# Spreading tokens into slots: 30 row masks with places of their own on GpSimd, and the clearing of `yo` and the identity behind them

## The chip, the cores and the metric

The kernel runs on one core of one Trainium2 chip. The metric is the device time of one execution in microseconds (us). The engines are TensorE (PE, with its weight loads PEld), VectorE (DVE), ScalarE (ACT), GpSimd (POOL) and SyncE (SP), which here only issues DMAs. Each works through its own instructions in order; semaphores tie them together.

## The reference

One layer of a streaming encoder over 2048 prompt tokens and 32 sample tokens, width 1024: a projection, a convolution group, stick-breaking attention, an output projection, and then a hierarchical mixture of experts, where the change lies. Each token picks one of 4 groups and two of its 8 experts; every expert is a SwiGLU block of hidden width 512.

```
lg = h @ w_rg; g_idx = argmax(lg); p_sel = softmax(lg)[g_idx]
le = (h @ w_re).reshape(T, 4, 8)[g_idx];  top_v, top_i = top_k(le, 2)
combine   = p_sel * softmax(top_v);  expert_id = g_idx * 8 + top_i
padded    = ceil(counts / 128) * 128                  # rows per expert, in blocks of 128
dest      = padded_start[expert] + rank within the expert
row_tok[dest] = token (T where empty);  row_w[dest] = combine weight
for each block of 128 rows, of expert e:
    y = (silu(x @ w_g[e]) * (x @ w_u[e])) @ w_d[e]
    out[row_tok] += y * row_w
```

## The kernel before

The program has three phases with a barrier between them: `phase_project`, `phase_attend` (its end also chooses experts and counts ranks, kept in `picks`) and `phase_moe`. Only `phase_moe` is touched.

`phase_moe` has an opening and then the experts. The opening turns, for each of 2080 tokens and two choices, the expert and the rank in it into a slot: block `col` and row `row` = rank mod 128. It is a *spread* by matmul: there are 34 pairs (2 choices by 17 tiles of 128 tokens). For each, a *row mask* (128 tokens by 128 rows, 1 where the token's row is that row) is the stationary operand and a *column mask* (128 tokens by 2 x 67 blocks, holding token number and weight at the token's block) the moving one; all 34 add up in the PSUM tile `up`, and give token and weight of every slot (`slots`).

- DVE first makes the table of the experts' first and last blocks (`nb`, `table`, L2090 to L2100), then casts `iota`, `tok` and `pad` (L2103 to L2105), then the row numbers (L2107 to L2110) and raises `rows_done`; then the column numbers (two products over 128x1088 and a sum, `oh`, `sel`, `col`), the weights (`vw`), and in the loop at L2128 the 34 column masks and every third row mask.
- POOL first makes the iotas, clears `yo` (L2197), builds the identity (L2198, L2200) and raises `zero_yo`; then it waits for `rows_done` and makes the other 23 row masks (L2210). Row and column masks have rings of `RS` = 6 buffers, so mask n waits until PE has done matmul n - 6. After `slots_done` it gathers the tokens of block 1 (it waits for `zeroed` there), then of block 2, and starts the scatter-adds to `y_out`.
- SP waits for `zero_yo`, stores the zeroed `yo` as the padding rows of `h2` and of `y_out` (semaphore `zeroed`), and then issues all weight loads, 12 pieces for each of 32 experts, in a ring of 16 buffers `raw`; a load waits until DVE has used the piece 16 before (`wlo_done`).
- ACT computes two exponentials, waits for `zero_yo`, then rounds the 12 pieces of expert 0 (`lead`, `w_hi`, L1949), and behind them rounds the transposed tokens of block 1 (`x_hi(1)`, L1953). DVE makes the remainders (`w_lo` L2152: five pieces, then `x_rest(1)` L2157, then the other seven).
- PE does the 34 matmuls (L1999), waits for `zero_yo`, transposes block 1 (L2007), and goes through the experts: per block `hidden` (up and gate, L2038), transposes of `h`, and `half_down` (L2027), three products for each pair of matrices.

No planner orders any of this; it is written out by hand, one queue per engine.

Of the kernel before, what the change touches and what calls it, by code (L numbers as in the profile page):

```python
# [16 lines left out]
P = 128  # L17
# [1800 lines left out]
def phase_moe(nc, io, scr, picks):  # L1818
# [6 lines left out]
    with ExitStack() as ctx:  # L1825
        def sb(name, shape, dt=F32):
            return ctx.enter_context(nc.sbuf_tensor("p3_" + name, shape, dt))
# [11 lines left out]
        NC = 2 * NT  # L1839
        se, psel, ex, den = (sb(x, [P, NT]) for x in ("se", "psel", "ex", "den"))  # L1840
        gx = sb("gx", [P, NT, NG])
# [8 lines left out]
        RS = 6  # L1850
        in_row, in_col = sb("in_row", [P, RS, P]), sb("in_col", [P, RS, 2, NBL])

# [32 lines left out]
        d_done, yo_done = sem("d_done"), sem("yo_done")  # L1885

        choices = [(k, r) for k in range(2) for r in range(NT)]
        pool_rows = [n for n in range(NC) if n % 3 < 2]

# [103 lines left out]
        def _(pe):  # L1993
            for n, (k, r) in enumerate(choices):
                m = DEC if ORDER[r] == PT else P
                if n in pool_rows:
                    pe.wait_ge(row_in, pool_rows.index(n) + 1)
                pe.wait_ge(spread_in, n + 1)
                pe.matmul(up[:, 0:2 * NBL], in_row[0:m, n % RS, :],  # L1999
                          in_col[0:m, n % RS, :, :].rearrange("p v b -> p (v b)"),  # L2000
                          start=(n == 0), stop=(n == len(choices) - 1)).then_inc(spread, 1)
# [71 lines left out]
        def _(dve):  # L2073
            links = [0]

            def link(ins):
                links[0] += 1
                ins.then_inc(chain, 1)
                dve.wait_ge(chain, links[0])

            def tt(out, a, b, op):
                link(dve.tensor_tensor(out, a, b, op))
# [4 lines left out]
            def flat(ap):  # L2087
                return ap.rearrange("p k t -> p (k t)")

            link(dve.tensor_scalar(nb[:, 0, :], picks.count, float(P - 1), None, ALU.add))  # L2090
            link(dve.tensor_copy(nbi[:, :], nb[:, 0, :]))
# [8 lines left out]
            dve.sem_inc(table_done, 1)  # L2100

            dve.wait_ge(consts, 5)
            link(dve.tensor_copy(iota[:, :], iota_i[:, :]))  # L2103
            link(dve.tensor_copy(tok[:, :], tok_i[:, :]))
            link(dve.tensor_copy(pad[:, :], pad_i[:, :]))  # L2105

            link(dve.tensor_copy(rki[:, :], flat(picks.rank)))  # L2107
            link(dve.tensor_scalar(rki[:, :], rki[:, :], 7, None, ALU.logical_shift_right))
            link(dve.tensor_copy(hi[:, :], rki[:, :]))
            link(dve.scalar_tensor_tensor(row[:, :], hi[:, :], -float(P), flat(picks.rank), ALU.mult, ALU.add))  # L2110
            dve.sem_inc(rows_done, 1)
            tt(oh[:, :, :], iota[:, 0:NE].unsqueeze(1).broadcast_to([P, NC, NE]), over(flat(picks.expert), NE),
# [6 lines left out]
            link(dve.tensor_reduce(se[:, :], gx[:, :, :], AX.X, ALU.add))  # L2119
            link(dve.reciprocal(psel[:, :], se[:, :]))  # L2120
            link(dve.tensor_scalar_add(den[:, :], ex[:, :], 1.0))
            link(dve.reciprocal(se[:, :], den[:, :]))
            for k in range(2):
                tt(vw[:, k * NT:(k + 1) * NT, 0], tok[:, :], row[:, k * NT:(k + 1) * NT], ALU.subtract)
            tt(vw[:, 0:NT, 1], se[:, :], psel[:, :], ALU.mult)
            tt(vw[:, NT:NC, 1], vw[:, 0:NT, 1], ex[:, :], ALU.mult)

            for n in range(NC):  # L2128
                if n >= RS:
                    dve.wait_ge(spread, n - RS + 1)  # L2130
                if n not in pool_rows:
                    dve.tensor_scalar(in_row[:, n % RS, :], iota[:, :], row[:, n:n + 1], None, ALU.is_equal)
                dve.scalar_tensor_tensor(in_col[:, n % RS, :, :],
                                         iota[:, 0:NBL].unsqueeze(1).broadcast_to([P, 2, NBL]), col[:, n:n + 1],
                                         vw[:, n, :].unsqueeze(2).broadcast_to([P, 2, NBL]), ALU.is_equal,
                                         ALU.mult).then_inc(spread_in, 1)
# [53 lines left out]
        def _(pool):  # L2190
            pool.iota(iota_i[:, :], pattern=[[1, P]], base=0, channel_multiplier=0).then_inc(consts, 1)
            at = ORDER.index(PT)
            for lo, n, first in ((0, at, 0), (at, 1, PT), (at + 1, NT - at - 1, at)):
                pool.iota(tok_i[:, lo:lo + n], pattern=[[P, n]], base=first * P - PAD,
                          channel_multiplier=1).then_inc(consts, 1)
            pool.iota(pad_i[:, :], pattern=[[0, 1]], base=PAD, channel_multiplier=1).then_inc(consts, 1)
            pool.memset(yo[:, :], 0.0).then_inc(consts, 1)  # L2197
            pool.memset(ident[:, :], 0.0).then_inc(ident_done, 1)  # L2198
# [5 lines left out]
            pool.sem_inc(zero_yo, 1)  # L2204

            pool.wait_ge(rows_done, 1)
            for n in pool_rows:
                if n >= RS:
                    pool.wait_ge(spread, n - RS + 1)
                pool.tensor_scalar(in_row[:, n % RS, :], iota[:, :], row[:, n:n + 1], None,  # L2210
                                   ALU.is_equal).then_inc(row_in, 1)

# [107 lines left out]
```

## Time and profile before

| what | us |
|---|---|
| median of 3 runs | 2269.47 (2268.47 to 2271.46) |
| the profiled execution | 2268.2 |
| its span, first to last instruction | 2266.5 |
| PE, DVE, ACT, POOL busy | 2132.9, 1634.1, 1296.8, 745.0 |
| third phase begins | 1350.0 |

Times inside the span count from its start. "busy" on PE is matmuls that overlap one another, so it says how rarely PE is empty, not how near to its peak it is. The chain that ended last takes 34% of the span on PE, 3% on ACT and 1% each on DVE and POOL in the page's own grouping. The opening of the third phase, from 1350.0 to the first expert matmul at 1387.3, is 37 us of the 2266.5.

### The profile page before, as it was taken

What the parts mean: (1) busy time and instruction counts of PE and PEld (TensorE: products, weight loads), DVE (VectorE), ACT (ScalarE), POOL (GpSimd) and SP (SyncE); (2) the same over time, 40 slices, a digit from 0 to 9 for tenths busy, and PEclk for the clock granted to TensorE, in tenths of its full rate; (3) what the DMA queues carried; (4) which work ended last, traced back from release to release, by engine and by line L of the source; (5) the groups of instructions that cost most, each with busy time, mean ns of one, the idle gap of its engine ahead of it and who ended that gap; (6) DMA issues with size and microseconds to landing.
All of it is one profiled execution on the core that took longest, in us unless ns stands there. A gap on an engine that the chain in (4) does not pass through costs nothing. (4 is left out here: it accounts for less than half of the span.)

```text
span 2266.5 us, 39757 instructions
## 1 busy us (share of the span) xinstructions
PE 2132.9 (94%) x13278; PEld 1790.1 (79%) x13279; DVE 1634.1 (72%) x2215; ACT 1296.8 (57%) x2417; POOL 745.0 (33%) x681
## 2 busy tenths in 40 slices
PE   8999999995899999899999857999999999999997
PEld 6888888884687887678778646888888888888886
DVE  3798999984676667877888868688688466466633
ACT  5222433335677677767767625588688465465533
POOL 1110444552466655544444423111111111111111
PEclk9999999996999999999999978999999999999999
DMA  6542433335433242332222129999899778678852
GB/s 219 198 163 85 137 118 112 118 115 176 120 103 106 80 140 75 107 110 91 78 101 71 61 88 342 331 334 377 290 377 375 247 231 273 219 236 278 276 171 46
DMA packets 209242, 406.60 MB, mean 179 GB/s; under 512 B 50623, under 2 KB 77119, under 8 KB 209117
## 3 DMA queue, kind: packets, MB, share of 16 engines
q1 hardware_dynamic: 195581, 355.71, 44.8%
q0 software_dynamic: 13536, 49.29, 9.2%
q8 instruction: 70, 1.15, 0.2%
q14 instruction: 55, 0.45, 0.1%
HBM read 312.27 MB, written 92.67 MB: 179 GB/s over the span
## 5 line engine op out<-in xcount | busy, mean ns | idle before, releaser
L2152 DVE TENSOR_TENSOR p_w_lo<-p_raw,p_w_hi 128x1024 fp32r<-128x1024 f32 x384 | 446.0, 1220 | 181.7 <-ACT p_w_hi L1949 181.0
L1792 POOL TENSOR_TENSOR p_wgt<-p_wgt,p_past 128x1024 f32<-128x1024 f32 (+4 forms) x166 | 308.4, 1859 | 350.5 <-DVE p_past L1670 347.4
L1949 ACT ACTIVATE p_w_hi<-p_raw 128x1024 fp32r<-128x1024 f32 x384 | 377.4, 1053 | 62.3 <-PE p_up L2038 51.8
L559 DVE SCALAR_TENSOR_TENSOR p_ut<-p_ut,p_cw 128x512 f32<-128x512 f32 (+1 forms) x480 | 329.2, 765 | 0.0
L1670 DVE TENSOR_TENSOR_SCAN p_past<-p_keep,p_past,p_one 128x513 f32<-128x513 f32 (+1 forms) x196 | 225.9, 1193 | 75.1 <-ACT p_keep L1481 73.1
L298 PE MATMUL p_pj<-p_w_hi,p_xt_hi 128*128 128x512 f32 x680 | 270.8, 398 | 4.2 <-DVE p_xt_lo L535 2.4
L298 PE MATMUL p_pj<-p_w_hi,p_xt_lo 128*128 128x512 f32 x680 | 266.3, 392 | 0.0
L298 PE MATMUL p_pj<-p_w_lo,p_xt_hi 128*128 128x512 f32 x680 | 265.8, 391 | 0.0
L1481 ACT ACTIVATE p_keep<-p_zp 128x512 f32<-128x512 f32 (+3 forms) x326 | 158.8, 547 | 118.1 <-PE p_zp L1351 105.4
L2038 PE MATMUL p_gp<-p_w_lo,p_xt_hi 128*128 128x256 f32 x736 | 206.7, 281 | 0.0
L2038 PE MATMUL p_gp<-p_w_hi,p_xt_lo 128*128 128x256 f32 x736 | 206.7, 281 | 0.0
L2038 PE MATMUL p_gp<-p_w_hi,p_xt_hi 128*128 128x256 f32 x736 | 206.6, 281 | 0.0
L1494 ACT ACTIVATE p_at<-p_tp 128x512 f32<-128x512 f32 (+3 forms) x261 | 134.2, 564 | 61.8 <-PE p_tp L1361 61.3
L2229 POOL DMA_INDIRECT y_out<-p_yo,p_at_s x47 | 75.5, 1606 | 284.1 <-ACT p_yo L1978 283.8
L1486 ACT ACTIVATE p_wgt<-p_zp 128x512 f32<-128x512 f32 (+3 forms) x326 | 160.2, 562 | 0.0
L1361 PE MATMUL p_tp<-p_ident,p_wgt 128*128 128x128 f32 x1106 | 151.4, 276 | 6.9 <-DVE p_at L1683 6.1
L1389 PE MATMUL p_op<-p_at,p_v 128*64 128x128 f32 x2176 | 155.2, 281 | 0.0
L2027 PE MATMUL p_dp<-p_w_hi,p_ht_hi 128*128 128x512 f32 x368 | 149.0, 405 | 4.3
L298 PEld LDWEIGHTS p_pj<-p_w_hi,p_xt_hi 128*128 128x128 f32 x680 | 128.3, 189 | 30.4 <-DVE p_xt_lo L535 2.8
L1670 DVE TENSOR_TENSOR_SCAN p_past<-p_keep,p_one 128x385 f32<-128x385 f32 (+3 forms) x130 | 113.9, 918 | 49.9 <-ACT p_keep L1481 46.2
L298 PEld LDWEIGHTS p_pj<-p_w_hi,p_xt_lo 128*128 128x128 f32 x680 | 128.1, 188 | 27.4
L2038 PE MATMUL p_up<-p_w_hi,p_xt_hi 128*128 128x512 f32 x368 | 146.3, 398 | 2.7 <-DVE p_xt_lo L2157 2.7
(268 smaller groups left out, 4713.2 us busy)
## 6 DMA issues: line engine op xcount, KB each, us to landing
p_raw<-in_w_up SPq DMA_DIRECT2D x128, 512.0 KB
p_raw<-in_w_gate SPq DMA_DIRECT2D x128, 512.0 KB
p_raw<-in_w_down SPq DMA_DIRECT2D x128, 512.0 KB
p_w_raw<-in_w_in SPq DMA_DIRECT2D x40, 256.0 KB, 3.8
p_x<-in_x SPq DMA_DIRECT2D x17, 512.0 KB, 4.1
p_y<-in_x SPq DMA_DIRECT2D x17, 512.0 KB
scr_y<-p_y SPq DMA_DIRECT2D x17, 512.0 KB, 3.0
p_y<-scr_y SPq DMA_DIRECT2D x17, 512.0 KB
```

The lines of the kernel that those rows point to most:

```text
L298: last = pe.matmul(pj[:, n % NPJ, :], xa[:, b, k, :], wa[:, place[c], k, :], start=(m == 0), stop=(m == 3 * KT - 1))
L559: dve.scalar_tensor_tensor(dst, src, cw[:, a, j:j + 1], dst, ALU.mult, ALU.add).then_inc(tap_done, 1)
L1361: end = pe.transpose(tp[:, n % 2, b * P:(b + 1) * P], wgt[:, u % NW, x * HW + b * P:x * HW + (b + 1) * P], ident[:, :])
L1389: end = pe.matmul(op[x * HD:(x + 1) * HD, pair * P:(pair + 1) * P], v_sb[:, key_slot(g, kt), h * HD:(h + 1) * HD], at[:, (base[u] + x) % N ...
L1481: act.activation(keep_rows[:, u % NK, x, HW - w:HW], zp[:, (base[u] + x) % NZ, 0:w], ACT.Sigmoid, scale=-SCALE).then_inc(keep_done, 1)
L1486: act.activation(wgt[:, u % NW, x * HW:x * HW + w], zp[:, (base[u] + x) % NZ, 0:w], ACT.Sigmoid, scale=SCALE).then_inc(sig_done, 1)
L1670: end = dve.tensor_tensor_scan(past[:, u % NP, to + w + 1:to:-1], src, one[:, 0:1].broadcast_to([P, w + 1]), past[:, (u - 1) % NP, to + 1: ...
L1792: pool.tensor_tensor(mine, mine, past_rows[:, u % NP, 0:n, 2:2 + w], ALU.mult).then_inc(a_done, 1)
L1949: act.activation(w_hi[:, p, :], raw[:, n % RING, :], ACT.Copy).then_inc(whi_done, 1)
L2027: last = pe.matmul(dp[:, c, :], ha[:, f, :], wa[:, KT + f, c * 512:(c + 1) * 512], start=(start and n == 0), stop=(not start and n == 5))
L2038: last = pe.matmul(dst, xa[:, k, :], wa[:, piece, at + lo:at + hi], start=(n == 0), stop=(n == 3 * KT - 1))
L2152: dve.tensor_tensor(w_lo[:, p, :], raw[:, n % RING, :], w_hi[:, p, :].bitcast(F32), ALU.subtract).then_inc(wlo_done, 1)
```

## The change

What it does:

- The 34 row masks lose their ring of six. There are 30 places: eight 128-column pieces of `xg`, eight of `yo`, four of `h`, four of `sg` and six of `in_rows`; mask n goes to place n mod 30. The tiles borrowed are used by the experts later. Column masks keep their ring of six.
- POOL makes 30 of the 34 row masks (`n % 7 < 6`) instead of 23, DVE 4 instead of 11. From mask 30 on POOL waits until matmul n - 30 is done.
- DVE works out the row numbers and casts `iota` first, raises `rows_done`, and then makes the table. `tok` and `pad` are cast after the column numbers. The weight is one reciprocal of (ex + 1) * se instead of two reciprocals and a product.
- POOL makes its masks right after the iotas. Clearing `yo` and building the identity, and with them `zero_yo`, stand behind the masks and a wait for the first 16 matmuls (the masks in `yo` have then been read). The code of SP and ACT is as it was.

```diff
--- before.py
+++ after.py
@@ -1837,7 +1837,7 @@
 
         iota_i, iota = sb("iota_i", [P, P], I32), sb("iota", [P, P])
         NC = 2 * NT
-        se, psel, ex, den = (sb(x, [P, NT]) for x in ("se", "psel", "ex", "den"))
+        se, ex, den = (sb(x, [P, NT]) for x in ("se", "ex", "den"))
         gx = sb("gx", [P, NT, NG])
         oh, sel = sb("oh", [P, NC, NE]), sb("sel", [P, NC])
         rki, hi = sb("rki", [P, NC], I32), sb("hi", [P, NC])
@@ -1848,7 +1848,7 @@
         nb, nbi = sb("nb", [P, 2, NE]), sb("nbi", [P, NE], I32)
         table = sb("table", [1, 2, NE], I32)
         RS = 6
-        in_row, in_col = sb("in_row", [P, RS, P]), sb("in_col", [P, RS, 2, NBL])
+        in_rows, in_col = sb("in_rows", [P, RS * P]), sb("in_col", [P, RS, 2, NBL])
 
         w_hi, w_lo = sb("w_hi", [P, PIECES, 2 * FF], F32R), sb("w_lo", [P, PIECES, 2 * FF], F32R)
         raw = sb("raw", [P, RING, 2 * FF])
@@ -1884,8 +1884,11 @@
         ht_ps, hh_done, hl_done = ([sem(f"{x}{i}") for i in range(2)] for x in ("ht_ps", "hh_done", "hl_done"))
         d_done, yo_done = sem("d_done"), sem("yo_done")
 
+        homes = [home[:, n * P:(n + 1) * P] for home, m in ((xg, 8), (yo, 8), (h, 4), (sg, 4), (in_rows, 6))
+                 for n in range(m)]
+        HOMES = len(homes)
         choices = [(k, r) for k in range(2) for r in range(NT)]
-        pool_rows = [n for n in range(NC) if n % 3 < 2]
+        pool_rows = [n for n in range(NC) if n % 7 < 6]
 
         block = ctx.enter_context(nc.Block())
 
@@ -1996,7 +1999,7 @@
                 if n in pool_rows:
                     pe.wait_ge(row_in, pool_rows.index(n) + 1)
                 pe.wait_ge(spread_in, n + 1)
-                pe.matmul(up[:, 0:2 * NBL], in_row[0:m, n % RS, :],
+                pe.matmul(up[:, 0:2 * NBL], homes[n % HOMES][0:m, :],
                           in_col[0:m, n % RS, :, :].rearrange("p v b -> p (v b)"),
                           start=(n == 0), stop=(n == len(choices) - 1)).then_inc(spread, 1)
 
@@ -2087,6 +2090,13 @@
             def flat(ap):
                 return ap.rearrange("p k t -> p (k t)")
 
+            link(dve.tensor_copy(rki[:, :], flat(picks.rank)))
+            link(dve.tensor_scalar(rki[:, :], rki[:, :], 7, None, ALU.logical_shift_right))
+            link(dve.tensor_copy(hi[:, :], rki[:, :]))
+            link(dve.scalar_tensor_tensor(row[:, :], hi[:, :], -float(P), flat(picks.rank), ALU.mult, ALU.add))
+            dve.wait_ge(consts, 5)
+            link(dve.tensor_copy(iota[:, :], iota_i[:, :]))
+            dve.sem_inc(rows_done, 1)
             link(dve.tensor_scalar(nb[:, 0, :], picks.count, float(P - 1), None, ALU.add))
             link(dve.tensor_copy(nbi[:, :], nb[:, 0, :]))
             link(dve.tensor_scalar(nbi[:, :], nbi[:, :], 7, None, ALU.logical_shift_right))
@@ -2098,17 +2108,6 @@
             link(dve.scalar_tensor_tensor(nb[0:1, 0, :], nb[0:1, 0, :], -1.0, nb[0:1, 1, :], ALU.add, ALU.add))
             link(dve.tensor_copy(table[0:1, 1, :], nb[0:1, 0, :]))
             dve.sem_inc(table_done, 1)
-
-            dve.wait_ge(consts, 5)
-            link(dve.tensor_copy(iota[:, :], iota_i[:, :]))
-            link(dve.tensor_copy(tok[:, :], tok_i[:, :]))
-            link(dve.tensor_copy(pad[:, :], pad_i[:, :]))
-
-            link(dve.tensor_copy(rki[:, :], flat(picks.rank)))
-            link(dve.tensor_scalar(rki[:, :], rki[:, :], 7, None, ALU.logical_shift_right))
-            link(dve.tensor_copy(hi[:, :], rki[:, :]))
-            link(dve.scalar_tensor_tensor(row[:, :], hi[:, :], -float(P), flat(picks.rank), ALU.mult, ALU.add))
-            dve.sem_inc(rows_done, 1)
             tt(oh[:, :, :], iota[:, 0:NE].unsqueeze(1).broadcast_to([P, NC, NE]), over(flat(picks.expert), NE),
                ALU.is_equal)
             tt(oh[:, :, :], oh[:, :, :], nb[:, 1, :].unsqueeze(1).broadcast_to([P, NC, NE]), ALU.mult)
@@ -2117,19 +2116,19 @@
 
             dve.wait_ge(exped, 1)
             link(dve.tensor_reduce(se[:, :], gx[:, :, :], AX.X, ALU.add))
-            link(dve.reciprocal(psel[:, :], se[:, :]))
-            link(dve.tensor_scalar_add(den[:, :], ex[:, :], 1.0))
-            link(dve.reciprocal(se[:, :], den[:, :]))
+            link(dve.scalar_tensor_tensor(den[:, :], ex[:, :], 1.0, se[:, :], ALU.add, ALU.mult))
+            link(dve.tensor_copy(tok[:, :], tok_i[:, :]))
+            link(dve.tensor_copy(pad[:, :], pad_i[:, :]))
             for k in range(2):
                 tt(vw[:, k * NT:(k + 1) * NT, 0], tok[:, :], row[:, k * NT:(k + 1) * NT], ALU.subtract)
-            tt(vw[:, 0:NT, 1], se[:, :], psel[:, :], ALU.mult)
+            link(dve.reciprocal(vw[:, 0:NT, 1], den[:, :]))
             tt(vw[:, NT:NC, 1], vw[:, 0:NT, 1], ex[:, :], ALU.mult)
 
             for n in range(NC):
                 if n >= RS:
                     dve.wait_ge(spread, n - RS + 1)
                 if n not in pool_rows:
-                    dve.tensor_scalar(in_row[:, n % RS, :], iota[:, :], row[:, n:n + 1], None, ALU.is_equal)
+                    dve.tensor_scalar(homes[n % HOMES], iota[:, :], row[:, n:n + 1], None, ALU.is_equal)
                 dve.scalar_tensor_tensor(in_col[:, n % RS, :, :],
                                          iota[:, 0:NBL].unsqueeze(1).broadcast_to([P, 2, NBL]), col[:, n:n + 1],
                                          vw[:, n, :].unsqueeze(2).broadcast_to([P, 2, NBL]), ALU.is_equal,
@@ -2194,6 +2193,14 @@
                 pool.iota(tok_i[:, lo:lo + n], pattern=[[P, n]], base=first * P - PAD,
                           channel_multiplier=1).then_inc(consts, 1)
             pool.iota(pad_i[:, :], pattern=[[0, 1]], base=PAD, channel_multiplier=1).then_inc(consts, 1)
+            pool.wait_ge(rows_done, 1)
+            for n in pool_rows:
+                if n >= HOMES:
+                    pool.wait_ge(spread, n - HOMES + 1)
+                pool.tensor_scalar(homes[n % HOMES], iota[:, :], row[:, n:n + 1], None,
+                                   ALU.is_equal).then_inc(row_in, 1)
+
+            pool.wait_ge(spread, 16)
             pool.memset(yo[:, :], 0.0).then_inc(consts, 1)
             pool.memset(ident[:, :], 0.0).then_inc(ident_done, 1)
             pool.wait_ge(ident_done, 1)
@@ -2202,13 +2209,6 @@
             pool.wait_ge(ident_done, 2)
             pool.wait_ge(consts, 6)
             pool.sem_inc(zero_yo, 1)
-
-            pool.wait_ge(rows_done, 1)
-            for n in pool_rows:
-                if n >= RS:
-                    pool.wait_ge(spread, n - RS + 1)
-                pool.tensor_scalar(in_row[:, n % RS, :], iota[:, :], row[:, n:n + 1], None,
-                                   ALU.is_equal).then_inc(row_in, 1)
 
             pool.wait_ge(slots_done, 1)
```

On POOL, at the opening of the third phase, before (`p_yo` and `p_ident` are the clearing and the identity, `p_in_row` the row masks, `p_at_g` and `p_xg` the first gather):

```order
L2191 IOTA p_iota_i 128x128
L2194 IOTA p_tok_i 128x6
L2194 IOTA p_tok_i 128x1
L2194 IOTA p_tok_i 128x10
L2196 IOTA p_pad_i 128x1
L2197 MEMSET p_yo 128x1024
L2198 MEMSET p_ident 128x128
L2200 AFFINE_SELECT p_ident<-p_ident 128x128
L2210 TENSOR_SCALAR p_in_row<-p_iota,p_row 128x128 x23
L2217 COPY p_at_g<-p_slots 128x1
L2219 DMA p_xg<-scr_h,p_at_g 128x1024
```

And now:

```order
L2195 IOTA p_pad_i 128x1
L2200 TENSOR_SCALAR p_xg<-p_iota,p_row 128x128 x7
L2200 TENSOR_SCALAR p_yo<-p_iota,p_row 128x128 x7
L2200 TENSOR_SCALAR p_h<-p_iota,p_row 128x128 x4
L2200 TENSOR_SCALAR p_sg<-p_iota,p_row 128x128 x3
L2200 TENSOR_SCALAR p_in_rows<-p_iota,p_row 128x128 x5
L2200 TENSOR_SCALAR p_xg<-p_iota,p_row 128x128 x4
L2204 MEMSET p_yo 128x1024
L2205 MEMSET p_ident 128x128
L2207 AFFINE_SELECT p_ident<-p_ident 128x128
L2217 COPY p_at_g<-p_slots 128x1
L2219 DMA p_xg<-scr_h,p_at_g 128x1024
```

The 30 masks have moved from behind the two memsets and the identity to ahead of them, and the masks' outputs are six tiles' pieces by turns.

On DVE, the start of the third phase, before (`p_nb`, `p_table` are the experts' table, `p_rki`, `p_hi`, `p_row` the row numbers; POOL's masks wait for the last of them and for `p_iota`):

```order
L2090 TENSOR_SCALAR p_nb<-picks 128x32
L2091 CAST p_nbi<-p_nb 128x32
L2092 TENSOR_SCALAR p_nbi<-p_nbi 128x32
...
L2099 CAST p_table<-p_nb 1x32
L2103 CAST p_iota<-p_iota_i 128x128
L2104 CAST p_tok<-p_tok_i 128x17
L2105 CAST p_pad<-p_pad_i 128x1
L2107 CAST p_rki<-picks 128x34
L2108 TENSOR_SCALAR p_rki<-p_rki 128x34
L2109 CAST p_hi<-p_rki 128x34
L2110 SCALAR_TENSOR_TENSOR p_row<-p_hi,picks 128x34
```

And now:

```order
L2093 CAST p_rki<-picks 128x34
L2094 TENSOR_SCALAR p_rki<-p_rki 128x34
L2095 CAST p_hi<-p_rki 128x34
L2096 SCALAR_TENSOR_TENSOR p_row<-p_hi,picks 128x34
L2098 CAST p_iota<-p_iota_i 128x128
L2100 TENSOR_SCALAR p_nb<-picks 128x32
L2101 CAST p_nbi<-p_nb 128x32
L2102 TENSOR_SCALAR p_nbi<-p_nbi 128x32
```

The row numbers and `p_iota` are the first five instructions instead of the last eight before the products.

## Rows read from the trace of the kernel before

**Rows 1.** Chain of waits, 1350 to 1430: start us, us, what
```profile
1375.21 1.09 PE p_up L1999 x6
...
1377.72 4.84 DMA p_xg<-scr_h,p_at_g
...
1387.27 7.26 PE p_up L2038 x24
...
1426.65 5.60 PE p_up L2038 x24
```

**Rows 2.** Windows, PE alone: stretch, its length, busy (instructions), granted clock, DMA share, GB/s
```profile
1400.00:1600.00 200.00, 196.39 (x1132) 1.00 0.98 342
1600.00:1800.00 200.00, 196.51 (x1157) 1.00 0.97 335
```

**Rows 3.** Timeline of ACT: start us, us, engine, line, operation [idle before, releaser]
```profile
1358.87 1.06 ACT L1949 ACTIVATE p_w_hi<-p_raw 128x1024 fp32r<-128x1024 f32 x1 [7.25 <-DMA p_raw<-in_w_up]
...
1373.64 1.06 ACT L1949 ACTIVATE p_w_hi<-p_raw 128x1024 fp32r<-128x1024 f32 x1 [0.25 <-DMA p_raw<-in_w_down]
1384.63 1.02 ACT L1953 ACTIVATE p_xt_hi<-p_xtp 128x1024 fp32r<-128x1024 f32 x1 [9.93 <-PE p_xtp L2007]
```

**Rows 4.** Timeline of SP's queue
```profile
1352.17 0.33 SPq L1910 DMA_DIRECT2D scr_h<-p_yo  x1
...
1353.02 3.19 SPq L1906 DMA_DIRECT2D p_raw<-in_w_up  x4
```

**Rows 5.** Timeline of POOL
```profile
1350.49 0.95 POOL L2197 MEMSET p_yo<- 128x1024 f32 x1
...
1351.77 0.29 POOL L2200 TENSOR_SCALAR_AFFINE_SELECT p_ident<-p_ident 128x128 f32<-128x128 f32 x1 [0.15 <-POOL p_ident L2198]
1354.83 4.29 POOL L2210 TENSOR_SCALAR p_in_row<-p_iota,p_row 128x128 f32<-128x128 f32 x4 [2.77 <-DVEq L2111]
1362.38 2.71 POOL L2210 TENSOR_SCALAR p_in_row<-p_iota,p_row 128x128 f32<-128x128 f32 x4 [3.26 <-PE p_up L1999]
1365.35 10.38 POOL L2210 TENSOR_SCALAR p_in_row<-p_iota,p_row 128x128 f32<-128x128 f32 x15 [0.26 <-PE p_up L1999]
```

**Rows 6.** Timeline of DVE
```profile
1350.50 0.98 DVE L2092 TENSOR_SCALAR p_nbi<-p_nbi 128x32 int32<-128x32 int32 x1
...
1353.16 0.23 DVE L2103 CAST p_iota<-p_iota_i 128x128 f32<-128x128 int32 x1
...
1353.82 0.18 DVE L2107 CAST p_rki<-picks 128x34 int32<-128x34 f32 x1
...
1354.47 0.20 DVE L2110 SCALAR_TENSOR_TENSOR p_row<-p_hi,picks 128x34 f32<-128x34 f32 x1
1354.82 1.29 DVE L2082 TENSOR_TENSOR p_oh<-p_iota,picks 128x1088 f32<-128x1088 f32 x1
...
1360.99 0.63 DVE L2133 SCALAR_TENSOR_TENSOR p_in_col<-p_iota,p_col,p_vw 128x134 f32<-128x134 f32 x2
```

**Rows 7.** Windows, PE alone, as rows 2
```profile
1361.00:1370.00 9.00, 8.50 (x36) 0.51 1.05 398
1370.00:1376.00 6.00, 5.42 (x34) 1.00 1.04 395
1387.00:1390.00 3.00, 2.73 (x7) 0.50 1.12 409
```

**Rows 8.** DMA issues: out<-in, queue, kind, count, KB, median us to landing
```profile
p_xg<-scr_h,p_at_g POOLq DMA_INDIRECT x47, 6.2
y_out<-p_yo,p_at_s POOLq DMA_INDIRECT x47, 9.0
...
y_out<-p_yo SPq DMA_DIRECT2D x1, 512.0 KB, 4.1
```

**Rows 9.** Masks by source, from 1365.6 and 1362: ns min/median/max, first and last start
```profile
L2133 DVE SCALAR_TENSOR_TENSOR p_in_col<-p_iota,p_col,p_vw x22: 344/351/462, 1365.4 to 1374.3; 128x134 f32<-128x134 f32 x22
...
L2210 POOL TENSOR_SCALAR p_in_row<-p_iota,p_row x19: 596/671/827, 1362.4 to 1375.1; 128x128 f32<-128x128 f32 x19
```

## The prediction

> **What bounds the kernel now.** I read the page first: TensorE (PE) is the engine with most busy time, and its matmul lines lead the chain. The change touches only the opening of the third phase (the experts), so the next view is the chain of waits from 1350 us on [rows 1]. It shows the phase opening with eleven microseconds of VectorE (DVE), then the spread (34 matmuls on PE, whose left operands, the row masks, come mostly from GpSimd, POOL), then the slot numbers, the gather of the first block's tokens, its transposition, the two halves of it (ACT, then DVE), and at 1387.27 the first expert matmul. From there on PE is what ends last: it is busy for 196.39 and 196.51 of the 200 us from 1400 and from 1600 [rows 2]. So a microsecond by which the first expert matmul moves is a microsecond of the kernel, but for at most 3.6 + 3.5 = 7.1 us of idle PE in those 400 us.
>
> Beside this chain runs a second one that the page does not list, because it ends earlier. ScalarE (ACT) rounds the first expert's 12 weight pieces (`lead`) before it does `x_hi(1)`, in one queue. The first of the 12 starts at 1358.87, the last at 1373.64, and `x_hi(1)` starts at 1384.63 [rows 3]: ACT has then been idle for 9.93 us. The 12 pieces come at 14.77 / 11 = 1.34 us each, although one takes ACT 1.06 us: the DMA sets the pace. Their loads are issued by SP from 1353.02, behind the two stores of the zeroed `yo` that begin at 1352.17 [rows 4], and SP starts all of this on `zero_yo`, which POOL raises when the memsets and the identity are done: memset of `yo` at 1350.49, identity finished at 1351.77 + 0.29 = 1352.06 [rows 5]. So the second chain has about ten microseconds of slack, and it hangs on POOL's clearing.
>
> **The change part by part.**
>
> *Row numbers first.* Before, POOL gets its first row mask at 1354.83, behind DVE's count chain, the three casts and the row numbers [rows 5, 6]. Now four operations 0.22 us apart, the last 0.2 long (1353.82 to 1354.67), and one cast of 0.26 (1353.16 to 1353.42) stand ahead: 1350.00 + 0.85 + 0.26 = 1351.1, and POOL starts 0.16 us later as it does before: 1351.3, 3.5 us earlier.
>
> *30 masks on POOL, none waiting for a buffer.* Before, POOL sits idle for 3.26 us before 1362.38 and 0.26 us before 1365.35, because the ring of six is full [rows 5]; that goes, since only the four masks from the 31st on still wait for PE, whose matmuls are long past. A mask on POOL takes 0.60 us at its shortest and 0.83 at its longest in the steady stretch [rows 9]. The first four, beside DVE's two 128x1088 products of 1.3 us, took 4.29 together, 1.9 more than 4 x 0.60; the last 15 in a row, beside the column masks, took 10.38, which is 0.692 each [rows 5, 6]. For 30: four around the products 4.3, about six more with DVE in small operations 3.6, and 20 at 0.692 13.8, together 21.7: the last mask ends at 1351.3 + 21.7 = 1373.0 where it ended at 1375.73. Bounds: 1371.2 if nothing but the products slows them (1.9 + 30 x 0.60 = 19.9), 1375.2 if the other 26 take 0.75 each, halfway between 0.67 (the median) and 0.83.
>
> *PE and DVE in the spread.* DVE's first column mask stood at 1360.99 [rows 6]. Ahead of it two small operations of some 0.25 us fall away, and 0.8 us of DVE's shift at 1350.50, which took 0.98 us beside POOL's memset where a like cast took 0.18: so PE can start near 1359.7. It has two matmul records per mask: 36 in the 9 us at the granted 0.51 (1.2 GHz), 34 in the 6 us at 2.4 GHz [rows 7], which is at most 0.50 and 0.35 per mask. About 18 go at half clock until 1368.7, 16 more take 5.6: PE could end at 1374.3, close behind POOL's last mask. I put the spread's end at 1374 instead of 1376.3 [rows 1]; that gain of some 2.3 us lies on the old chain only. DVE, with seven masks fewer, is no bound.
>
> *Clearing and identity behind the masks.* Nothing in SP's or ACT's code moves, but both open with a wait for `zero_yo`, and it now comes behind 30 masks. The clearing takes 1.57 us (1350.49 to 1352.06), so `zero_yo` comes at 1373.0 + 1.6 = 1374.6 instead of 1352.06: 22.5 us later. Queued behind that wait on SP are the two zero stores and all weight loads; on ACT the 12 roundings and `x_hi(1)`; PE waits for it too, after the spread. What waits for SP's stores is the gather (`zeroed`): the slower one lands 4.1 us after issue [rows 8], so at about 1375 + 4.1 = 1379, and gather 1 goes out about 1379.6, not 1377.72 [rows 1]. With 6.2 us to landing and the 2.07 us from there (1382.56) to `x_hi(1)`, the transposes, the block is there at 1388: still ahead of ACT.
>
> ACT's last rounding ended at 1373.64 + 1.06 = 1374.70 and so ends at 1374.70 + 22.5 = 1397.2 if the DMAs run as before. They do not quite: gather 1, gather 2 (out at about 1388.5) and the first scatter-add (about 1390) now fall into the same stretch, where before they came after it. A piece of 128x1024 numbers costs 1.34 us of the DMA's pace and a gather moves as many. Bounds: one such transfer (1.3) and four, counting the scatter-add twice (5.3). I take two and a half, 3.3, since the two gathers fall wholly and the scatter-add, 9.0 us to landing, partly, ahead of the last piece. So `x_hi(1)` starts at 1397.2 + 3.3 = 1400.5 instead of 1384.63: 15.9 us later. What follows is the same code: x_rest, PE, and DVE's second seven pieces, which stand behind x_rest and shift with it.
>
> *The clock.* The first 24 expert matmuls took 7.26 us where 24 later ones took 5.60 [rows 1], because the granted clock was 0.50 (1.2 GHz) for their first 3 us [rows 7]: 1.7 us. Now PE idles about twelve microseconds between the transposes and that point. The other low stretch in the rows, nine microseconds from 1361 after about 15 of idling, would do half the work and cost 4.5. So the extra lies between 0 and 2.8; I take 1.0, nearer to the row of the same matmuls.
>
> Sum: 15.9 + 1.0 = 16.9 us slower. The profiled execution took 2268.2 (span 2266.5 and 1.7 around it): 2285.1. The median of the runs is 1.3 us higher, 2269.47, so a median of about 2286.
>
> **The rivals.**
>
> *POOL is shut out by every column mask.* The masks beside the 1.3 us products lost 1.9 us, and DVE's shift beside the memset 0.8 [rows 5, 6]: the two engines do hold each other up. If each column mask of DVE, which reads two operands from SBUF as the products do, kept POOL out for its whole length, the 20 masks from 1359.8 on and the 34 column masks of 0.35 us would stand in line: 12.0 + 11.9 = 23.9 us, the last mask at 1383.7, `zero_yo` 10.7 us later still, 2297 for a median. Against it: from 1365.35 to 1375.73 POOL made 15 masks while DVE made 22 column masks [rows 9]; one after the other they need 15 x 0.60 + 22 x 0.35 = 16.7 us and had 10.4. 3%. The rule behind this rival is in the Trainium skill (SBUF — State Buffer, section on the two separate sides): VectorE and GpSimd share one port pair under an exclusive lock, which a VectorE operation with two SBUF inputs holds against a reading GpSimd operation for all of its length. The trace agrees with it for the long products (1.9 us lost) and not for the column masks (10.4 us where the rule needs 16.7).
>
> *Part is given back.* PE's 7.1 us of idle up to 1800 could shrink if what it waits for there runs on while PE is late. Against it: those waits are for ACT's and DVE's work on the running block, which shifts with it. At most 2286 - 7 = 2279. 6%.
>
> *The weight stream stays behind.* Loads start 22.5 us later and PE only 17, so the second expert's pieces may come late. By pace, the first 28 pieces (two experts and the third's up-weights) and eight other transfers need 36 x 1.34 = 48 us from 1375, until 1423. Before, PE began the third block's up-matmuls at 1426.65 [rows 1] and would now at 1443: a wide margin, unless the ring's releases chain badly: then 3 to 8 us more, 2289 to 2294. 6%.
>
> *The loads stay hidden: not slower.* Then only the old chain counts, with the spread's end 2.3 us earlier: 2269.47 - 2.3 = 2267. It decides where the 12 pieces are rounded within the 7 us or so between `zero_yo` at 1374.6 and the transposes, 0.6 us each; DMA gave 1.34 and ACT alone takes 1.06. Only if `zero_yo` came by about 1362 would the slack cover it, and 30 masks of 0.60 from 1351.3 exclude that. 3%, mostly for something I misread.
>
> That the masks are not made faster (POOL slowed all along) would not save the case: a spread that ends later makes `zero_yo` later too.
>
> **How the numbers follow.** 82% for the forecast with its own terms: low with the masks through at 1371.2 (1.8 less), one transfer (2.0 less) and no extra clock (1.0 less) 12.1, which is 2280.3 by the profiled execution; high with 1375.2 (2.2 more), four transfers (2.0 more) and 2.8 of clock (1.8 more) 22.9, which is 2291.1 by it and 2292.4 for a median. This range also holds most of the stream rival and some of the give-back; the lock rival stays out. About 0.2%, 4.5 us, is what a measurement can tell here from no change. Faster by more: 2%, within: 2%, slower: 96%.
>
> **What would show it.** In the changed profile: POOL's first mask near 1351.3, its last near 1373; memset of `yo` right behind it; SP's first store near 1375; ACT's 12 roundings from about 1381.5 to 1400, in a row, with idle time that ended with `p_raw` DMAs; the chain of waits through weight DMA and L1949 instead of the gather; the first expert matmul at 1403, at half clock; equal idle time of PE afterwards. It is wrong if ACT's `x_hi(1)` stands before 1395, if SP's loads start before POOL's masks are through, or if PE's idle time after 1400 (on the shifted scale) falls by several microseconds.

## The result and the profile after

The changed kernel takes 2283.62 us (median of 6 runs, 2282.68 to 2286.20), the kernel before 2269.43: a ratio of 1.0068 (95% interval 1.0057 to 1.0078), 14.2 us slower by the medians. (The ratios in this document are the estimates on record with their intervals, not the quotient of two medians; that is 1.0063 here and lies inside the interval.) The prediction was 2286, between 2280.3 and 2292.4. The profiled execution took 2282.77, its span is 2281.1.

One thing has to be known before the traces are laid side by side. The first two phases, whose code is the same, do not take equally long in every execution: the third phase begins at 1349.97 in the trace of before and at 1348.79 in that of after, and between 1348.40 and 1352.58 in those of the experiments. So I read everything from the start of the third phase (POOL's first iota), and compare *the length of the third phase*, span minus that start: 2266.5 - 1350.0 = 916.5 us before, 2281.1 - 1348.8 = 932.3 after, 15.8 us longer.

POOL's timeline after (start us, us, engine, line, operation) answers to [rows 5]:

```profile
1348.79 0.24 POOL L2190 IOTA p_iota_i<- 128x128 int32 x1 [15.88 <-POOLq L2260]
...
1350.15 6.06 POOL L2200 TENSOR_SCALAR p_xg<-p_iota,p_row 128x128 f32<-128x128 f32 x7 [0.78 <-DVEq L2099]
1356.19 4.13 POOL L2200 TENSOR_SCALAR p_yo<-p_iota,p_row 128x128 f32<-128x128 f32 x7
...
1367.82 2.64 POOL L2200 TENSOR_SCALAR p_xg<-p_iota,p_row 128x128 f32<-128x128 f32 x4
1370.41 0.95 POOL L2204 MEMSET p_yo<- 128x1024 f32 x1
...
1371.65 0.42 POOL L2207 TENSOR_SCALAR_AFFINE_SELECT p_ident<-p_ident 128x128 f32<-128x128 f32 x1
...
1377.61 1.26 POOL L2219 DMA_INDIRECT p_xg<-scr_h,p_at_g  x1 [0.64 <-POOL p_at_g L2217]
```

The masks start 1.36 us into the phase (4.86 before) and run without a gap to 21.67 (25.76 before); the clearing follows, and `zero_yo` comes at 1372.07, 23.3 us into the phase instead of 2.1. SP's queue follows at once [rows 4]:

```profile
1372.17 0.33 SPq L1913 DMA_DIRECT2D scr_h<-p_yo  x1
1372.54 0.43 SPq L1914 DMA_DIRECT2D y_out<-p_yo  x1
1373.02 3.18 SPq L1909 DMA_DIRECT2D p_raw<-in_w_up  x4
```

And ACT [rows 3], whose 9.93 us of idle time before `x_hi(1)` are gone:

```profile
1378.72 1.06 ACT L1952 ACTIVATE p_w_hi<-p_raw 128x1024 fp32r<-128x1024 f32 x1 [28.28 <-DMA p_raw<-in_w_up]
...
1394.30 1.06 ACT L1952 ACTIVATE p_w_hi<-p_raw 128x1024 fp32r<-128x1024 f32 x1 [0.86 <-DMA p_raw<-in_w_down]
1397.37 1.06 ACT L1952 ACTIVATE p_w_hi<-p_raw 128x1024 fp32r<-128x1024 f32 x1 [2.01 <-DMA p_raw<-in_w_down]
1398.33 1.01 ACT L1956 ACTIVATE p_xt_hi<-p_xtp 128x1024 fp32r<-128x1024 f32 x1
```

`x_hi(1)` now starts directly behind the last of the 12 roundings, and that one waited 2.01 us for its DMA. The chain of waits after (start us, us, what), where [rows 1] had the gather, now runs through the masks, the clearing, SP's queue and the weight load:

```profile
1370.46 0.89 POOL p_yo L2204
...
1382.05 0.52 SPq L1909
1382.62 14.73 DMA p_raw<-in_w_down
...
1398.33 1.02 ACT p_xt_hi L1956
1399.37 1.24 DVE p_xt_lo L2156
1400.61 0.34 issue
1400.95 8.28 PE p_up L2041 x24
```

The first 24 expert matmuls take 8.28 us instead of 7.26. Windows of PE (length, busy, granted clock, DMA share, GB/s) show the clock in that place, and PE's busy time later, 14 us on from the windows of [rows 2]:

```profile
1398.00:1401.00 3.00, 0.05 (x1) 0.50 1.02 383
1401.00:1404.00 3.00, 3.00 (x7) 0.50 1.04 391
1404.00:1407.00 3.00, 3.00 (x10) 0.61 1.06 391
```
```profile
1414.00:1614.00 200.00, 196.41 (x1135) 1.00 0.99 348
1614.00:1814.00 200.00, 196.55 (x1157) 1.00 0.96 333
```

196.41 and 196.55 where it was 196.39 and 196.51: nothing is given back later. From the phase's start, the first expert matmul moved from 37.30 to 52.16 us, 14.9 later, and the 24 took 1.0 longer: together 15.9, which accounts for the phase's 15.8. What follows the 24 takes 872.0 us before and 871.9 after, and between 871.6 and 872.4 in the traces of all the experiments: everything that differs between these kernels lies ahead of that point.

### The profile page after: what moved, and what is told of

Same layout as the page of the kernel before. It is cut to its first block and busy times, and to the rows that moved or that the text cites. A ratio compares the mean times of both kernels' runs of the same rounds, so it can differ in the third digit from the quotient of the medians.

```text
span 2281.1 us, 39763 instructions
## 1 busy us (share of the span) xinstructions
PE 2130.4 (93%) x13278; PEld 1788.8 (78%) x13279; DVE 1632.3 (72%) x2206; ACT 1298.4 (57%) x2417; POOL 746.1 (33%) x688
## 5 line engine op out<-in xcount | busy, mean ns | idle before, releaser
L2217 POOL COPY p_at_g<-p_slots 128x1 int32 (+1 forms) x47 | 9.5, 201 | 428.8 <-PE p_xtp L2010 424.0
```

## Experiments

The table has for each kernel the median, and from its trace, in us from the start of the third phase: SP's first store (just behind `zero_yo`), the last rounding's end, `x_hi(1)`, the first expert matmul; then the spread's end and the phase's length. In the edits, comment lines and `...` stand for code that is left out.

```
kernel                      median    store  rounded  x_hi(1)  matmul  spread  phase
before                      2269.43    2.20    24.7    34.7     37.3    26.3   916.5
after                       2283.62   23.38    49.6    49.5     52.2    24.1   932.3
1  clearing first           2267.11    2.25    24.7    32.9     35.6    24.7   915.5
2  before, clearing last    2286.46   26.16    52.1    52.0     54.6    25.1   935.1
3  loads ahead of the wait  2274.15   23.43    21.6    39.6     42.2    24.1   922.1
4  second gather late       2282.38   23.39    47.1    47.0     49.7    23.9   929.6
5  clearing at mask 10      2271.58   10.74    33.6    36.1     38.7    25.4   917.7
6  clearing at mask 20      2277.27   17.06    41.0    40.9     43.5    24.0   923.4
7  after, PE kept busy      2285.62   23.60    50.0    49.9     52.6    23.1   931.6
8  clearing first, PE busy  2264.48    2.25    25.0    32.5     35.1    24.2   912.7
9  split 23 and 11          2268.27    2.25    25.0    33.0     35.7    24.3   916.7
10 row numbers late         2268.56    2.19    25.0    34.1     36.8    25.6   915.9
```

There is one trace for each kernel, and two stretches in it differ between traces for no reason in the code. The first 24 expert matmuls take 7.26 to 8.63 us in the ten kernels whose TensorE is given no extra work, depending on when the granted clock rises from 0.50 (some 3 us after their start in the kernel before, some 5 in the first experiment); three kernels that leave TensorE idle for the same 2.7 us just ahead of them (the first, ninth and tenth) have 8.07, 8.60 and 7.53. The spread ends at 24.1 in three traces and at 23.1 in a fourth (the seventh), with the same masks made by the same engines in the same order. So a difference of less than about 1.4 us in the phase, or 1 us in the spread, is not shown by these traces alone; the column `matmul` is free of the first of the two.

### 1: the clearing first, all else as changed

```diff
-        in_rows, in_col = sb("in_rows", [P, RS * P]), ...
+        in_rows, in_col = sb("in_rows", [P, 14 * P]), ...
-        ... ((xg, 8), (yo, 8), (h, 4), (sg, 4), (in_rows, 6))
+        ... ((xg, 8), (h, 4), (sg, 4), (in_rows, 14))
 # POOL: memset yo, memset ident, affine_select, zero_yo
-# behind the 30 masks and wait_ge(spread, 16)
+# ahead of wait_ge(rows_done, 1) and the 30 masks
```

> The changed kernel with the clearing of yo and the identity ahead of the masks again; the eight places in yo are replaced by eight more in a tile of their own, so all 30 places, the 30:4 split and DVE's new order stay. My theory (the late zero_yo delays the weight loads, and nothing else in the change costs time): the loads start 3 us into the phase, are hidden, and only the faster spread is left: the first mask about 2.2 us into the phase, the last mask about 23, the spread's end about 24.5 instead of 26.3: 2267.5, 1.5 to 2 us below the kernel before. Rival (30 masks on GpSimd, or the borrowed places, cost the time): 2278 or more.

Measured: 2267.11 beside 2268.84 for the kernel before on the same chip, ratio 0.9993 (0.9984 to 1.0002). The interval holds no change; the phase is 1.0 us shorter than before, which is within the scatter, and 16.8 shorter than the changed one. First mask at 2.4, last mask's end at 22.3, spread's end at 24.7: within 0.7 us of what was expected. ACT waits for the transposes again, as in the kernel before:

```profile
1382.14 1.02 ACT L1956 ACTIVATE p_xt_hi<-p_xtp 128x1024 fp32r<-128x1024 f32 x1 [8.20 <-PE p_xtp L2010]
```

So 30 masks on POOL and the 16 places that are still borrowed cost nothing; the place of the clearing, which the eight places in `yo` force, costs all of it. The first matmul is 1.7 us earlier than before, and 0.8 of that goes again, since the first 24 take 8.07 us.

### 2: the kernel before with nothing but the clearing moved

```diff
+            # wait for rows_done, 23 masks
             pool.memset(yo[:, :], 0.0).then_inc(consts, 1)
             ...
             pool.sem_inc(zero_yo, 1)
-            # wait for rows_done, 23 masks
```

> The kernel before with one edit: the clearing and the identity, with zero_yo, moved behind its 23 masks. My theory: masks end 25.7 us into the phase, zero_yo at 27.3, the last rounding 26.4 later at 53.7, x_hi(1) 19 us later than before, and 1 us of half clock: 2289.5. Rival (the new masks cost the time, not the clearing): 2269 to 2270.

Measured: 2286.46, ratio 1.0073 (1.0057 to 1.0089), the phase 18.6 us longer than before. One edit, none of the rest, and the slowdown is there, with ACT waiting for a load up to the last piece:

```profile
1402.28 1.06 ACT L1949 ACTIVATE p_w_hi<-p_raw 128x1024 fp32r<-128x1024 f32 x1 [1.71 <-DMA p_raw<-in_w_down]
```

The phase grew by 1.4 us less than the 20.0 that 2289.5 stands for (the medians on this chip differ by 17.6). Most of this is that `zero_yo` came at 26.1, not 27.3: without the memset beside it DVE finishes the row numbers 0.8 us earlier, and 15 masks took 9.95 us instead of 10.38.

### 3: the late `zero_yo` kept, the first loads taken out of its wait

```diff
+            load(0, 0)
             sp.wait_ge(zero_yo, 1)
             ...stores...
-            for a in range(4):
+            for a in range(1, 4):
                 load(0, a)
 # ScalarE
-            act.wait_ge(zero_yo, 1)
-            act.sem_inc(yo_done, 1)
             lead((0, 0), 0, PIECES)
+            act.wait_ge(zero_yo, 1)
+            act.sem_inc(yo_done, 1)
```

> The changed kernel with its order on GpSimd, but SP issues the first expert's 12 loads ahead of its wait for zero_yo, and ScalarE rounds them ahead of its own. My theory: the loads are all that zero_yo costs. The stores of zeros and the first gather then set the end: zero_yo at 23.3 us of the phase, stored at 28, gather out at 28.3 instead of 27.7 before: 2270, within 1.5 us of the kernel before. Rival (the late stores and the late gather cost as much as the weights): 2276 or more.

Measured: 2274.15, ratio 1.0026 (1.0017 to 1.0036); the phase is 5.6 us longer than before and 10.2 shorter than after. Neither value was met. The weights are the larger part, but with them out of the way `x_hi(1)` is still 4.9 us later than before, where I had expected 0.5. POOL's timeline there shows why:

```profile
1377.15 1.02 POOL L2218 COPY p_at_g<-p_slots 128x1 int32<-128x1 int32 x1 [4.72 <-DMA y_out<-p_yo]
1378.47 1.92 POOL L2220 DMA_INDIRECT p_xg<-scr_h,p_at_g  x1 [0.30 <-POOL p_at_g L2218]
```

The copy waits 4.72 us for the store to land, then takes 1.02 instead of 0.19, and the gather's issue takes 1.92 instead of 1.26, both inside a run of DVE's two-operand `w_lo` products. The issue starts 1.6 us later in the phase than before, and the gather then lands 8.2 us after it (4.84 in [rows 1]): 3.3 of the 4.9. In that stretch SP is loading the second expert's pieces, and the DMA engines move 397 GB/s, against 190 while the gather before is under way. In the first and ninth experiments, at 301 and 344 GB/s, it takes 4.8 and 5.3. That the loads are the cause is read from these rates and was not tried by itself. PE begins the transposes at 37.6 us of the phase, before at 32.7.

### 4: the second gather and the first scatter-add out of the weights' stretch

```diff
             end = pool.value_load(...)
+            pool.wait_ge(xh_done, 2)
             gather(2)
             add(0)
```

> The changed kernel with GpSimd waiting for x_hi(1) before the second gather and the first scatter-add, so these two stay out of the stretch in which the 12 weight pieces land. In the changed kernel the 12 pieces took 26.4 us from zero_yo to the last rounding's end, before 22.6: 3.7 more. My theory (transfers of GpSimd's queue take the DMA engines from the weights, 1.3 us for each 512 KB): only gather 1 is left, 24.0 us, and 2281.2. Rival A (the 3.7 has another cause, such as gather 1 alone): 2283.6, no change. Rival B (second gather too late for the second block): 2284 or more.

Measured: 2282.38, ratio to the kernel before 1.0060 (1.0046 to 1.0074). The medians alone would not tell it from the changed kernel; the traces do. The first store to the last rounding's end takes 23.7 us, after 26.3, and before 22.5, and the phase is 2.7 us shorter (2.4 expected; 2.5 of it is the earlier first matmul). The last pieces come with 0.22 us of wait each:

```profile
1395.84 1.06 ACT L1952 ACTIVATE p_w_hi<-p_raw 128x1024 fp32r<-128x1024 f32 x1 [0.22 <-DMA p_raw<-in_w_down]
1397.12 1.06 ACT L1952 ACTIVATE p_w_hi<-p_raw 128x1024 fp32r<-128x1024 f32 x1 [0.22 <-DMA p_raw<-in_w_down]
```

where the changed kernel had 0.86 and 2.01. So the two transfers cost 2.5 us. The remaining 1.2 is put down to gather 1 by subtraction; the sixth experiment has 1.4 in the same place (23.9 from store to last rounding).

### 5 and 6: the clearing behind 10 and behind 20 masks

```diff
             for n in pool_rows:
+                if n == pool_rows[10]:      # pool_rows[20] in the sixth
+                    # memset yo, memset ident, affine_select, zero_yo
```

> The first experiment's kernel (14 places of its own, none in yo) with the clearing, the identity and zero_yo behind GpSimd's first 10 masks. My theory (the weight stream is hidden as long as it ends before the gathered block is transposed, and each microsecond beyond that counts one): zero_yo at 10.8 us of the phase; the last rounding could end 22.6 later at 33.4, and with gather 1 sharing the DMA engines at about 35 where x_hi(1) stood at 33.0: 2 to 3 us above the first experiment, 2269.5. Rival (any delay of zero_yo counts in full, 8.7 us): 2276.

> The same behind GpSimd's first 20 masks. My theory: zero_yo at 17.5 us of the phase, the last rounding's end at 40.1 plus 1 to 3 us for the gathers, 42, so 9 us above the first experiment: 2276. Rival (the delay counts in full, 15.4 us): 2282.5. Rival (one step, not a slope: any clearing behind masks costs what all 30 cost): 2283.6.

Measured: 2271.58 (ratio 1.0013, 1.0004 to 1.0022) and 2277.27 (1.0041, 1.0025 to 1.0056); the phases are 2.2 and 7.9 us longer than in the first experiment, for a `zero_yo` that is 8.5 and 14.8 us later. It is neither one step nor a full count. By the first expert matmul, which is free of the scatter of the 24, the first 8.5 us of delay cost 3.1, the next 6.3 cost 4.8, and the last 6.3, up to all 30 masks, 8.7. In the fifth the roundings still end (33.6) before `x_hi(1)` starts (36.1). Of the 3.1 us by which that starts later, 0.7 are the spread's later end, and 2.4 the gather, which takes 7.19 us instead of 4.77 while the DMA engines carry weights (404 GB/s instead of 301). In the sixth `x_hi(1)` follows the last rounding directly. There the second gather and the scatter-add are issued 4.4 and 3.0 us before the last rounding starts and leave no wait in it (0.23 us); in the changed kernel they are issued 9.0 and 7.5 us before, and the way from store to last rounding is 2.4 us longer. 6.3 and 2.4 make the 8.7; that the 2.4 is the two transfers' is what the fourth experiment shows.

I had expected rises of 2 to 3 and of 9 over the first experiment; by the phases they are 2.2 and 7.9. By the medians, each set against the kernel before on its own chip, they are 4.4 and 10.1, and 2271.58 is 2.1 above the expected 2269.5.

### 7 and 8: TensorE kept busy where it was idle

```diff
+            def warm(n):
+                for _ in range(n):
+                    pe.matmul(dp[:, 0, 0:P], iota[:, :], iota[:, :], start=True, stop=True)
+            warm(20)                    # 0 in the seventh; ahead of the spread
             ...the 34 matmuls...
+            warm(16)                    # 0 in the seventh
             pe.wait_ge(zero_yo, 1)
             transpose_x(1)
+            warm(6)                     # 32 in the seventh
```

The seventh is the changed kernel with these, the eighth the first experiment's.

> The changed kernel with 32 matmuls of iota by iota (results unused) on TensorE between the first block's transposes and the first expert matmul, where it is idle for 13.9 us. My theory (the first 24 expert matmuls take 8.28 us and not 5.60 because the clock is at its lower level, so the idle time has a price of its own): they take 5.6 to 6, and the kernel 2.5 us less, 2281. Rival (they are slow for want of remainders from VectorE or of loads): 8.3 as before and no change, 2283.6.

> The first experiment's kernel with such matmuls in all of TensorE's idle time of the opening: 20 ahead of the spread, 16 ahead of the transposes, 6 behind them. My theory: the spread is 0.6 us shorter (VectorE's column masks then set its pace), the transposes 1 us, the first 24 expert matmuls 2.4 us: 4 us below the first experiment, 2263, below both kernels. Rival (the clock doesn't rise for matmuls so small, or they delay the spread): no faster than the first experiment, 2267.

Measured for the seventh: 2285.62, ratio 1.0080 (1.0066 to 1.0094), not 2281: no gain (its phase is 0.7 us shorter than the changed kernel's, which is within the scatter). The chain and PE's windows:

```profile
1403.77 7.12 PE p_up L2047 x24
```
```profile
1397.00:1400.00 3.00, 1.48 (x14) 1.00 1.07 282
1400.00:1403.00 3.00, 0.00 (x0) 1.00 1.03 353
1403.00:1406.00 3.00, 2.23 (x5) 0.53 1.05 399
```

The 32 matmuls took only 8.9 us, since the clock rose on the way. They ended 5.29 us before the first expert matmul, and when that began the granted clock was at 0.50 (1.2 GHz) again. The 24 took 7.12 us instead of 8.28, just below the 7.26 to 8.63 of the other kernels. The test missed its aim by ending too soon.

The eighth does not: 2264.48, ratio 0.9980 (0.9971 to 0.9989), the phase 3.8 us shorter than before and 2.8 shorter than in the first experiment. The chain there:

```profile
1361.78 12.53 PE p_up L2008 x68
1374.88 3.81 PE p_dp L1999 x32
1381.52 1.08 PE p_xtp L2016 x8
1385.26 5.85 PE p_up L2047 x24
```

The 24 take 5.85 us at a granted 1.00, against 8.07 in the first experiment and at least 7.26 in any kernel without such matmuls: 2.2 us of the 2.8. The spread's end is 0.5 earlier, which is within its scatter. The transposes take 1.08 us instead of 1.95, but start 0.4 later in the phase, so little of that arrives. This version is 0.2% faster than the kernel before (0.1% to 0.3%), the only one here that is clearly so.

### 9 and 10: which part of the change made the spread shorter

```diff
-        pool_rows = [n for n in range(NC) if n % 7 < 6]     # the ninth
+        pool_rows = [n for n in range(NC) if n % 3 < 2]
```
```diff
+            # the tenth, VectorE: the table of experts (10 operations), table_done
             # row numbers, iota, rows_done
-            # the table of experts (10 operations), table_done
```

Both start from the first experiment.

> The first experiment's kernel with the old split of the row masks, 23 on GpSimd and 11 on VectorE, each still with a place of its own. In the first experiment TensorE went through its 34 matmuls from 11.6 to 24.7 us of the phase without a wait for GpSimd. My theory (TensorE at half clock sets the spread's pace, so the places and the earlier row numbers brought the gain, and the 30:4 split did not): the spread ends within 0.5 us of that, and the kernel is unchanged, 2267. Rival (VectorE with 11 masks becomes the bound, 34 x 0.35 + 11 x 0.3 = 15.2 us): the spread ends 1.5 us or more later.

> The first experiment's kernel with VectorE's old order: the table of experts first, then row numbers and iota. My theory (GpSimd's chain of 30 masks at 0.65 to 0.68 us sets the end if it starts late): first mask at about 4.4 us of the phase instead of 2.4, last mask's end at 24.6 instead of 22.3, the spread's end 0.6 to 1.2 us later, 2268. Rival (GpSimd's start has 2 us of slack, since TensorE starts on VectorE's first column mask): no change in the spread's end.

Measured: 2268.27 and 2268.56, ratios 0.9997 (0.9987 to 1.0006) and 1.0001 (0.9991 to 1.0010), so the times say nothing and the traces have to. With 23 masks on POOL, the last is done at 17.7 us of the phase, and the spread ends at 24.3, no later than with 30 (24.7): the split brings nothing. With the row numbers late, the masks run from 4.5 to 25.1, PE waits for them, and the spread ends at 25.6, 1.0 us later, as expected. A wait for the last masks is in the trace (0.16 us ahead of the last three of them), so this is more than scatter. Of the 1.7 us by which the spread ends earlier than before, this is 1.0; the other 0.7 is left to the places and the shorter weight computation, which were not tried apart.

## Why the prediction was right

*The second chain.* The step on which all rests held: `zero_yo` holds back SP's and ACT's queues, ten microseconds of slack cover part, and the rest is the kernel's. The first two experiments show it from both sides (all of the change but this: no longer than before; nothing but this: 18.6 longer).

*The terms*, in us from the phase's start, prediction and trace: first mask 1.3 and 1.36; last mask's end 23.0 and 21.7; `zero_yo` 24.6 and 23.3; last rounding's end 50.5 and 49.6; the extra of the clock 1.0 and 1.0. The sum was 16.9 and is 15.8 by the phase. None of the three signs of being wrong came: `x_hi(1)` stands at 1398.33, the loads start behind the masks, and PE's idle time later is the same. The profiled executions differ by 14.6, because the phase began 1.2 us earlier in that of after; the medians differ by 14.2.

*The mis-sized term* is the 30 masks: 21.7 us forecast and 20.3 measured. I took 0.692 us for each of 20; in the trace the five in `in_rows` take 3.15 us, 0.63 each. The ninth experiment has 0.61 with 11 masks on DVE, so it is not that DVE makes fewer. In the two kernels with the ring of six, where every mask waits on a semaphore, they take 0.69 and 0.66; whether the wait is the difference was not tried. (The upper bound for the masks, 1375.2, should read 1375.1: 4.3 and 26 x 0.75 make 23.8.)

*The DMA's share.* 3.3 us forecast for two and a half transfers. From `zero_yo` to the last rounding's end the trace has 26.4 us against 22.6: 3.7. The fourth experiment shows 2.5 of it as the work of the second gather and the scatter-add.

*The clock.* That the 24 matmuls are slow because of the clock is shown by the windows and by the eighth experiment, where they take 5.85 us at full clock. The forecast of 1.0 for the *longer idle time* fits by luck. The first experiment has TensorE idle for 2.67 us ahead of them, as before (2.68), and they take 8.07 us; the changed kernel, after 13.92 us of idling, 8.28. So 0.8 of the 1.0 comes without the cause that I gave, and the kernel before, on whose 7.26 the term was built, is the fastest of the ten without filler.

*The spread's end* was put at 24.0 and is 24.1, by two errors that cancel: PE starts 10.95 us into the phase, not 9.7, and needs 13.1 us, not 14.6. It lies on the old chain and has no part in the sum.

*The lock rival* failed in the changed kernel as in the rows: 30 masks beside 34 column masks in 20.3 us. *Given back* and *stream behind* failed too: PE's busy time later is the same to 0.04 us in 200, and all that follows the first 24 matmuls to 0.1 in 872.

*The old chain behind the late stores.* I had the block ready at 38 us of the phase; the transposes end at 38.3, 11 us ahead of the last rounding's end, so it stays clear as the prediction says. The gather went out at 28.8, not 29.6, and took longer than the 6.2 us I gave it. What failed is the expectation for the third experiment, where this chain alone sets the end: 4.9 us late, not 0.5.

## What to carry to other kernels

Before instructions are moved behind others on an engine, list the semaphores that they raise and every queue that opens with a wait on them: here three small operations that looked like housekeeping held 12 weight loads. Count the slack of the chain that is *not* shown in the list of what ended last, since that chain takes over from there: here the first 8.5 us of delay cost 3.1, and at the end each further one cost more than one (8.7 us for 6.3), because the delayed loads also met other transfers. If the borrowed space forces the order, give up the borrowing of that one tile before the order.

## What the runs showed that I had not expected

- Transfers on POOL's queue and on SP's slow each other both ways, as far as these traces tell: a gather that lands in 4.84 us at 190 GB/s takes 7.5 us at 386 (changed kernel, from 1377.61 to the transposes at 1385.07) and 8.2 us at 397 (third experiment), and the second gather with a scatter-add takes 2.5 us from the loads.
- POOL's own part of a gather can stretch inside a run of DVE's products over 128x1024: the copy from 0.19 to 1.02 us, the issue from 1.26 to 1.92 (third experiment). It need not: in the kernel before, the issue and a run of the same products both start at 1377.72, and the issue takes 1.26.
- In the seventh experiment the granted clock was at 0.50 when the expert matmuls began, 5.3 us after the last matmul before them; in the eighth, 1.3 us after, it was at 1.00.
- With the clearing first, a cast of DVE's in the row numbers that runs beside POOL's memset takes 0.98 us, 0.8 more than usual, in the first experiment's timeline of DVE:

```profile
1349.52 0.18 DVE L2094 TENSOR_SCALAR p_rki<-p_rki 128x34 int32<-128x34 int32 x1
1349.74 0.98 DVE L2095 CAST p_hi<-p_rki 128x34 f32<-128x34 int32 x1
```
- The start of the third phase differs by up to 4.2 us between profiled executions of kernels whose first two phases are the same code, more than the effects of one or two that half of the experiments look for; only measured from the phase's start do the traces show those, and only down to the scatter said above.
